# Second attention's units taken in pairs of heads from both partition halves, with their 64-row logits issued alternately

## The reference

```python
logit_s = jnp.einsum('bqgrd,bgqkd->bgrqk', qf, ks) + bias_s
p_s = masked_softmax(logit_s, (rel_s >= 0)[:, :, None])
o_s = jnp.einsum('bgrqk,bgqkd->bqgrd', p_s, vs)
...
logit_w = jnp.einsum('bqgrd,bkgd->bgrqk', qf, kw) + bias_t[:, :, t5_bucket(rel_w)]
p_w = masked_softmax(logit_w, mask_w)
o_w = jnp.einsum('bgrqk,bkgd->bqgrd', p_w, vw)
o = gb[..., 0:1] * o_c + gb[..., 1:2] * o_s + gb[..., 2:3] * o_w
```

## Time and profile before

| | |
|---|---|
| median of 3 runs | 3264.51 us (3263.86 to 3267.88) |
| the profiled execution | 3261.71 us |
| its span, first to last instruction | 3259.9 us |
| PE busy | 2782.5 us, 85% of the span |
| DVE busy | 1667.5 us, 51% |
| ACT busy | 837.0 us, 26% |
| mean granted clock of TensorE | 0.929 of full speed |
| the attention loop, from its first logits to the first part behind it | 1467.3 to 1601.0 us of the span |

### The profile page before, as it was taken

How to read it: one execution, slowest core, us unless ns; L and a number is a source line. 1 busy time by engine, 2 the same in 40 slices (tenths; PEclk the granted TensorE clock), 3 DMA queues, 4 the chain that set the end, 5 groups by cost and what they waited for, 6 DMA issues and landing times.

```text
span 3259.9 us, 32744 instructions
## 1 busy us (share of the span) xinstructions
PE 2782.5 (85%) x12704; PEld 1998.1 (61%) x12704; DVE 1667.5 (51%) x2452; ACT 837.0 (26%) x1219; POOL 697.3 (21%) x647
## 2 busy tenths in 40 slices
PE   4999999999999999979987088778887787777779
PEld 4888789988999888777786033333333333333347
DVE  3444455544455554434557955555455555555544
ACT  3444444443444444314442000000000000000023
POOL 0000000000000000000000255555554655555500
PEclk9999999999999999878998598988989899889889
DMA  5445455555565556512341599999999999999963
GB/s 175 155 143 168 137 186 181 181 194 194 183 185 189 191 185 220 143 55 77 124 140 48 206 388 421 422 422 422 422 422 414 422 422 422 422 422 422 422 239 117
DMA packets 234671, 839.68 MB, mean 258 GB/s; under 512 B 21691, under 2 KB 29195, under 8 KB 168252
## 3 DMA queue, kind: packets, MB, share of 16 engines
q0 software_dynamic: 73728, 536.90, 39.6%
q1 hardware_dynamic: 154188, 298.44, 28.0%
q10 hardware_dynamic: 6640, 2.70, 0.3%
HBM read 835.86 MB, written 2.13 MB: 257 GB/s over the span
## 4 chain that ended last, share of the span: by engine, by line
PE 62%; DMA 13%; DVE 9%; issue 7%; POOL 6%; ACT 2%; ACTq 1%; POOLq 0%; DVEq 0%
DMA big<-in_peer_u,idxc 13%; PE bank L1744 12%; PE bank L1354 8%; PE bank L1357 7%; PE bank L1356 7%; PE bank L1376 7%; PE bank L1378 7%; PE bank L1380 7%; DVE big L1283 2%; POOL idxc L1790 2%; POOL big L1799 2%; POOL vrows L1806 1%; PE bank L1566 1%; PE bank L1689 1%; PE bank L1691 1%
## 5 line engine op out<-in xcount | busy, mean ns | idle before, releaser
L1744 PE MATMUL bank<-vrows,eacc 128*128 128x512 f32 x2048 | 1002.1, 650 | 355.8 <-DVE eacc L1296 355.6
L808 DVE TENSOR_TENSOR wl<-raw,wh 128x1024 fp32r<-128x1024 f32 (+1 forms) x544 | 653.3, 1210 | 775.6 <-ACT wh L489 775.5
L1744 PEld LDWEIGHTS bank<-vrows,eacc 128*128 128x128 f32 x2048 | 418.6, 209 | 939.2 <-issue 674.9
L1283 DVE CUSTOM_DVE_ANT_0 big<-big,tmp 128x2048 f32<-128x2048 f32 x256 | 576.4, 2290 | 584.7 <-DMA big<-in_peer_u,idxc 584.5
L489 ACT CAST wh<-raw 128x1024 fp32r<-128x1024 f32 (+1 forms) x544 | 559.9, 1036 | 799.6 <-PE bank L1357 427.8
L1376 PE MATMUL bank<-Ah,wh 128*128 128x256 f32 x1792 | 508.7, 284 | 5.0 <-DVE Al L798 5.0
L1378 PE MATMUL bank<-Al,wh 128*128 128x256 f32 x1792 | 507.8, 283 | 0.0
L1380 PE MATMUL bank<-Ah,wl 128*128 128x256 f32 x1792 | 507.8, 283 | 0.0
L1376 PEld LDWEIGHTS bank<-Ah,wh 128*128 128x128 f32 x1792 | 344.9, 192 | 5.7 <-issue 5.6
L1378 PEld LDWEIGHTS bank<-Al,wh 128*128 128x128 f32 x1792 | 344.8, 192 | 0.1
L1380 PEld LDWEIGHTS bank<-Ah,wl 128*128 128x128 f32 x1792 | 344.8, 192 | 0.0
(11 more groups left out here) (241 smaller groups left out, 2322.3 us busy)
## 6 DMA issues: line engine op xcount, KB each, us to landing
raw<-in_mlp_w SPq DMA_DIRECT2D x128, 1024.0 KB, 5.3
raw<-in_sb_w_qkv SPq DMA_DIRECT2D x48, 1024.0 KB, 5.2
raw<-in_w_in SPq DMA_DIRECT2D x28, 1024.0 KB, 5.0
raw<-in_sb_w_o SPq DMA_DIRECT2D x16, 1024.0 KB, 5.0
raw<-in_w_out SPq DMA_DIRECT2D x16, 1024.0 KB, 5.1
raw<-in_peer_w_q SPq DMA_DIRECT2D x16, 1024.0 KB, 5.0
raw<-in_ple_w_gate SPq DMA_DIRECT2D x16, 1024.0 KB, 5.0
big<-in_peer_u,idxc POOLq DMA_INDIRECT x256, 13.2
```

The costliest lines, as they stand in the source:

```text
L808: V_.tensor_tensor(wlv[hq % 4][:, :, 0:width], raw_half[hq][:, :, 0:width], whf[hq % 4][:, :, 0:width], ALU.subtract).then_inc(split_done, 1)
L1283: V_.tensor_tensor_reduce(out=ubuf[g][b], in0=ubuf[g][b], in1=xn[:, m, :], scale=1.0, scalar=0.0, op0=ALU.mult, op1=ALU.add, accum_out=hcu ...
L1744: mm = nc.tensor.matmul(banks[4 * m + n][:, :], diag[g][b], vbuf[g][b][:, n * 512:n * 512 + 512], start=False, stop=last and g == GROUPS - ...
```

## The change

The 32 units are renumbered and taken as 16 *pairs*. Units 2p and 2p + 1 are the same head number r and the same q of two groups, one in each partition half (g = 0 with 1, then 2 with 3). Their logits are four matmuls issued as b = 0 lower half, b = 0 upper half, b = 1 lower, b = 1 upper; the lower half always writes bank 6 and the upper bank 7. The wait ahead of them changes with it: before, unit u waited for DVE to have read unit u - 2; now pair p waits for DVE to have read all of pair p - 1. The loops have 20 (PE) and 21 steps of a pair each; transposes come one step after the logits, values two steps after, one part in each step.

Two head groups now fill at the same time, the lower half's in bank 2 and the upper's in bank 3, and both are finished together. So the row sums and reciprocals get four slots, `group_out` runs twice in a row every fourth step, and `out_turn`, `out_hi` and `out_lo` run for two g in a row, at two places instead of four. The first values of the next two head groups wait for both `group_out`s.

```diff
@@ PE
-            def att_logits(u):
-                g, q, r, gq = att_unit(u)
-                rows = slice((g % 2) * DK, (g % 2 + 1) * DK)
+            def att_logits(p):
+                j, q, r = p // 8, p // 4 % 2, p % 4
                 w = P * (q + 1)
-                if u >= 2:
-                    pe.wait_ge(s_ready, u - 1)
+                if p:
+                    pe.wait_ge(s_ready, 2 * p)
                 for b in range(2):
-                    mm = nc.tensor.matmul(banks[6 + u % 2][:, b * S:b * S + w], qTa[rows, R * (g // 2) + r, q * P:(q + 1) * P],
-                                          kTn[rows, b, g // 2, 0:w], start=True, stop=True)
-                mm.then_inc(lg_done, 1)
+                    for l in range(2):
+                        rows = slice(l * DK, (l + 1) * DK)
+                        mm = nc.tensor.matmul(banks[6 + l][:, b * S:b * S + w], qTa[rows, R * j + r, q * P:(q + 1) * P],
+                                              kTn[rows, b, j, 0:w], start=True, stop=True)
+                        if b:
+                            mm.then_inc(lg_done, 1)
...
@@ PE, att_values
-                if r == 0 and gq < 2:
-                    pe.wait_ge(co_taken[1], gq + 1)
+                if u < 2:
+                    pe.wait_ge(co_taken[1], u + 1)
                 elif r == 0:
-                    pe.wait_ge(o_added, gq - 1)
+                    pe.wait_ge(o_added, 2 * (u // 8))
                 for b in range(2):
-                    o = banks[2 + gq % 2][:, b * S + r * DK:b * S + (r + 1) * DK]
+                    o = banks[2 + u % 2][:, b * S + r * DK:b * S + (r + 1) * DK]
...
@@ PE, the loop
-            for s in range(40):
-                if s < 32:
+            for s in range(20):
+                if s < 16:
...
-                if 2 <= s < 34:
-                    att_turn(s - 2)
-                if s >= 13 and (s - 13) % 8 == 0:
-                    out_turn((s - 13) // 8)
-                if 3 <= s < 35:
-                    att_values(s - 3)
-                if s % 2 and s < 33:
-                    wout_part(s // 2)
+                for u in (2 * s - 2, 2 * s - 1):
+                    if 1 <= s < 17:
+                        att_turn(u)
+                if s in (11, 19):
+                    for g in (s // 8 * 2 - 2, s // 8 * 2 - 1):
+                        out_turn(g)
+                for u in (2 * s - 4, 2 * s - 3):
+                    if 2 <= s < 18:
+                        att_values(u)
+                if 1 <= s < 17:
+                    wout_part(s - 1)
@@ DVE, the loop
-                if s < 32:
-                    logits(s)
...
-                if s >= 7 and (s - 7) % 4 == 0 and s < 36:
-                    group_out((s - 7) // 4)
-                if s >= 14 and (s - 14) % 8 == 0:
-                    out_lo((s - 14) // 8)
-                if s >= 3 and s % 2 and s < 35:
-                    wout_conv(4 + (s - 3) // 2)
+                for u in (2 * s, 2 * s + 1):
+                    if s < 16:
+                        logits(u)
...
+                if s >= 6 and (s - 6) % 4 == 0:
+                    for l in range(2):
+                        group_out((s - 6) // 4, l)
+                if s in (12, 20):
+                    for g in (s // 8 * 2 - 2, s // 8 * 2 - 1):
+                        out_lo(g)
+                if 2 <= s < 18:
+                    wout_conv(s + 2)
@@ the order of units and of the transpose banks
-    return u // 8, u // 4 % 2, u % 4, u // 4
+    return 2 * (u // 16) + u % 2, u // 8 % 2, u // 2 % 4, 2 * (u // 8 % 2) + u % 2
-    return u + max(0, (u - 4) // 8)
+    return u + (2 if u >= 22 else 0)
-    return turn_use(min(8 * g + 11, 31)) + 1
+    return 22 + g if g < 2 else 32 + g
```

More of the change, by code:

```diff
@@ L666, in exps @@
             def exps(u):
-                g, q, r, gq = att_unit(u)
+                g, q, r, slot = att_unit(u)
                 act.wait_ge(s_ready, u + 1)
                 for b in range(2):
-                    sums = 8 + 8 * (gq % 2) + 4 * b + r
+                    sums = 8 + 8 * slot + 4 * b + r
                     nrm_max = 2 * (u % 4) + b
@@ L693, in _ @@
                 wout_conv(w)
-            for s in range(40):
-                if s < 32:
-                    exps(s)
+            for s in range(21):
+                for u in (2 * s, 2 * s + 1):
+                    if s < 16:
+                        exps(u)
                 if s == 1:
@@ L700, in _ @@
                         nc.scalar.copy(ob[:, 0, n * 512:n * 512 + 512], banks[n][:, :]).then_inc(co_taken[0], 1)
-                if 2 <= s < 34:
-                    take_turned(s - 2)
-                if s >= 13 and (s - 13) % 8 == 0:
-                    out_hi((s - 13) // 8)
-                if s >= 3 and s % 2 and s < 35:
-                    wout_conv(4 + (s - 3) // 2)
+                for u in (2 * s - 2, 2 * s - 1):
+                    if 1 <= s < 17:
+                        take_turned(u)
+                if s in (11, 19):
+                    for g in (s // 8 * 2 - 2, s // 8 * 2 - 1):
+                        out_hi(g)
+                if 2 <= s < 18:
+                    wout_conv(s + 2)
             act.wait_ge(o_split, 4)
@@ L1123, in logits, with group_out @@
                 last.then_inc(s_ready, 1)
[L1125 to L1130, removed]
+            def group_out(jq, l):
+                g, q, slot = 2 * (jq // 2) + l, jq % 2, 2 * (jq % 2) + l
+                c = nrm[:, 40 + 8 * slot:48 + 8 * slot]
+                dve.wait_ge(e_ready, 16 * jq + 14 + 2 * l)
+                link(V_.reciprocal(c, nrm[:, 8 + 8 * slot:16 + 8 * slot]))
                 g0 = q * WIN_REST + 12 * g
@@ L1134, in group_out @@
                 link(V_.tensor_tensor(c2, c2, gate, ALU.mult))
-                dve.wait_ge(pv_done, 4 * gq + 4)
-                link(V_.tensor_tensor(ot, banks[2 + gq % 2][:, :].rearrange("p (n d) -> p n d", n=8),
+                dve.wait_ge(pv_done, 8 * jq + 7 + l)
+                link(V_.tensor_tensor(ot, banks[2 + l][:, :].rearrange("p (n d) -> p n d", n=8),
                                       c.unsqueeze(2).broadcast_to((P, 8, DK)), ALU.mult))
@@ L1149, in out_lo @@
                     "p (c s) -> p c s", c=2), Ahf[:, 8 + 2 * g:10 + 2 * g, :], ALU.subtract).then_inc(o_split, 1)
-            for s in range(40):
-                if s and s % 8 == 0 and s <= 32:
-                    n = s // 8 - 1
+            for s in range(21):
+                if s >= 5 and (s - 5) % 4 == 0 and s <= 17:
+                    n = (s - 5) // 4
                     add_to_scaled_tile(used(J_WOUT - 1) + 4 * (n + 1), A_WOUT + 2 * n, n, rfin)
-                if s < 32:
-                    logits(s)
+                for u in (2 * s, 2 * s + 1):
+                    if s < 16:
+                        logits(u)
                 if s == 1:
@@ L1648, in out_turn @@
                 t = out_turn_use(g)
-                pe.wait_ge(o_added, 2 * g + 2)
+                pe.wait_ge(o_added, 4 * (g // 2) + 3 + g % 2)
                 turn_bank_free(t)
```

1 line of the change is left out of this document (removed).

## The result

The changed kernel takes 3280.47 us (median of 5 runs, 3279.28 to 3283.26), the kernel before 3263.86 us beside it (5 runs, 3257.15 to 3267.88). The ratio, which is estimated from all the runs and not from the two medians, is 1.0055, its 95% interval 1.004 to 1.007: slower, by 16.6 us in the median. Predicted were 3276 us, in a range from 3268 to 3287. The profiled execution took 3279.28 us against 3261.71, its span is 3277.5 us against 3259.9.

What follows compares the result with a forecast made beforehand. PE was taken to bound the attention loop. Gains of 14.9 us against waits of 15.9, 3.8, 0.9 and 1.3 gave +7.0, with the clock +11.8 us: 3273.5, forecast as 3276 us for the median, range 3268 to 3287.

Steps and rivals of the forecast that it cites:

- The switches: PE's way into 64-row work and out again: 16 visits instead of 32, 15 x 0.335 = 5.0 us saved.
- The alternation: Logits passes of the two halves run beside each other, eight in the time of four: 9.9 us saved.
- the halves don't overlap: Rival: a pair's logits passes share no time, so the 9.9 us aren't gained; 3283.5 us, chance 0.14.
- The three waits: PE, before values of units 8, 16, 24, waits for both `group_out`s: 13.2 us, 15.9 with DVE's lateness.
- the 1.9 us of lateness in step 6: DVE reaches the pair's logits late because its conversion waits for ACT, adding some 1.9 us to PE's first wait.
- The bank waits: PE waits for banks at `out_turn` in step 11 and transposes in step 12: 3.8 us more than before.
- the start: At the loop's start the second pair's logits wait for DVE and delay the compressed branch: 0.9 us net.
- the end: At the loop's end two `group_out`s stand where one did, and PE's work moves: some +1.3 us.
- The clock: Half clock on PE behind each of three new long idle times costs 1.6 us, 4.8 us in all.
- the clock holds: Rival: transposes and values break up the waits, PE stays at full clock, +7.0 us, 3271.5 us; chance 0.14.
- addition of 0.1 us for each change of half: Without overlap, each change of half in the logits costs a third of a switch: 4.5 us more, 3288 us.
- The waits aren't there: Rival: both `group_out`s end before PE has issued the pair's transposes; sum -8.9 us, 3255.6 us, chance 0.04.

Runs made afterwards that it cites:

- same_half: Changed kernel with the upper half's logits computed from the lower half's rows, so all of a pair's passes lie in one half; 3291.84 us, ratio 1.0080.
- group_out_early: Changed kernel with both `group_out` calls one step earlier on DVE and each unit's values waiting only for their own bank's; 3262.72 us, ratio 0.9978.
- the pair without waits: Changed kernel with earlier `group_out`s, own-bank waits and moved `out_turn`, `out_hi`, `out_lo`: 3254.65 us; the same with upper logits from lower rows: 3261.93 us.
- half_by_half: Changed kernel with a pair's four logits matmuls issued as both of the lower half, then both of the upper; 3281.17 us, ratio 1.0051.
- kept_warm: Changed kernel with six matmuls of zeros, 384 columns each, ahead of each of the three waits for `group_out`; 3275.35 us, ratio 1.0027.
- own_wait: Changed kernel with each unit's values waiting for their own bank's `group_out` instead of both; 3281.95 us, ratio 1.0038.

## Why the prediction was right, and where it was off

- **That PE bounds the loop**: held. same_half's 10.3 us more work lengthened the loop by 8.7, group_out_early's 14.6 us less waiting with the 6.7 of clock that went with it, shortened it by 21.3; DVE is busy for 64.8 us of 148.2 and ACT for 60.0.
- **The switches, 5.0 us**: 6.5 us by before less same_half. Part of this may be more than the switches; the runs don't split it further.
- **The alternation, 9.9 us, all of it**: 10.3 us by same_half less after, 9.6 in the pair without waits. The rival that the halves don't overlap is refuted: four passes' time for eight.
- **The three waits, 4.4 + 1.9, 4.35, 4.4 + 0.8**: 6.21, 4.45 and 5.01 us, so 15.7 for 15.9. DVE's two `group_out`s behind the pair's logits and its lateness from ACT's conversion are both in its timeline. But the 1.9 us of lateness in step 6 doesn't follow from its working: 7.3 - 5.7 - 0.95 + 0.3 is 1.0. It came to 1.9 all the same (logits 2.85 us behind the pair's first pass, at 1514.68 against 1511.83, instead of 0.95), because DVE's chain of step 5, 7.3 us as predicted, began 1.4 us behind PE's step (1507.41 against 1506.01) and not 0.3. That this term fits is luck.
- **The bank waits, 1.9 and 1.95 + 0.45**: 2.04 and 2.25 + 0.2. The start's single wait of 3.46 and the end's 2.86 + 0.85 complete the 27.3 us of idle time. At the start PE waited 1.8 + 0.5 before (its matmuls; the 2.06 of the earlier trace rows is the idle time of its loads), so it is 1.2 more where 0.9 were predicted; at the end 3.06 before, so 0.65 more where 1.3 were. The whole difference is 21.0 for 21.9.
- **The clock, 3 x 1.6 = 4.8**: this is the step that was mis-sized. It measured 10.2 us. The price was taken from one short idle time at the end of the loop, where 3.43 us of passes were slowed. Behind the three waits PE was busy for 5.96, 4.79 and 5.83 us at 0.50, half of it 8.3 us. The two waits of some 2 us, which I left without price, were followed by 3.41 us, 1.7 more, and the end by 0.6 more; the start gave 0.4 back. With these the sum is 10.2.
- **The rivals**: without the clock the loop would be 4.3 us longer (21.0 - 16.7), with it 14.5, so "the clock holds" is refuted by its own number. "The halves don't overlap" is refuted by same_half, and so is its addition of 0.1 us for each change of half: alternating has three changes in a pair and half_by_half one, which would be 3.0 us over 15 pairs, and their work differs by 0.2. "The waits aren't there" is refuted by the first row of the waits, and turned into a kernel by group_out_early: with the waits gone the pair of gains stays, which is why it is faster.
- **The number**: 3280.5 for 3276. The loop brought +14.5 instead of +11.8, and 3.1 us lie outside it; against that the median is 1.2 us above the profiled execution, not 2.8. In the loop the clock term was 5.4 too small, and too little gain (1.8) and too much wait (0.9) made up half of it. That the errors have opposite signs is luck.

Pairing itself is right: 16.7 us of PE work saved. What made it slower is that two `group_out`s come at once on DVE behind logits issued in the same step, and what a wait of PE does to its clock afterwards.

## What to carry to other kernels

When units are regrouped so that two results are finished together, look at once at who waits for both, and move their consumer to the step that produces them: here that, with each bank waiting for its own result, was worth 21 us, more than the 16.7 of the regrouping. Price a new wait of TensorE at its length plus half of what it does at half clock behind it, read from the stretches, and don't count on a shorter wait unless the clock stays up. 64-row products in different halves only have to be at hand together: for the four matmuls of a pair here their order made no difference.

## What the hardware showed that was not expected

- The clock fell not only behind the long waits. Behind 2.04 us and, 5.8 us of work later, 2.25 us, it was 0.50 for 3.41 us; in group_out_early the same 2.25 us, 9 us behind another wait, had none. Behind the 2.27 us left over in kept_warm it was 0.50 for 6.82 us, and the wait of 2.04 us, followed by full clock in after, had 3.41 us at half clock there. So neither the length of the wait alone nor its share tells here whether it drops.
- A stretch can also be at 1.00 while PE is mostly idle: 1.44 us busy of 3.41 in own_wait, and full clock; then 0.50 in the next, where PE was busy for 6.76 of 6.83 us.
- The Trainium skill (TensorE: Matmul & The Clock Gate, "Packing small matmuls — row/col tiling") has matmuls start strictly in program order. half_by_half doesn't agree: by that rule only the last lower and the first upper pass could share their time, so the pair would take three passes more than it did, 3 x 0.215 = 0.65 us. It took 1.08 us, against 1.07 when alternating.
